# More expert-value blocks as full float32 products, and side-token dot products moved from the u stage into the v stage

## The reference, cut to what matters

```python
def peer(x, w_q, sub_keys, u, v):                 # once per layer, T = 256 tokens, D = 1024
    q = (xt @ w_q).reshape(T, 8, 2, 128)
    s = einsum('thpd,pnd->thpn', q, sub_keys)     # scores of 2 x 128 sub-keys per head
    sv, si = top_k(s, 16)
    cand = sv[:, :, 0, :, None] + sv[:, :, 1, None, :]
    cv, ci = top_k(cand.reshape(T, 8, 256), 16)
    experts = (i1 * 128 + i2)                     # 8 x 16 = 128 experts of 16384 per token
    gates = softmax(cv)
    a = gelu(einsum('td,tkd->tk', x, u[experts])) * gates
    return einsum('tk,tkd->td', a, v[experts])
```

## Time and profile before

| | us |
|---|---|
| median of 3 runs | 1658.11 (1657.31 to 1663.31) |
| the profiled execution, its own time | 1663.31 |
| its span, first to last instruction | 1661.5 |
| PE busy | 1628.2 (98%) |
| DVE busy | 1323.9 (80%) |
| ACT busy | 651.8 (39%) |
| POOL busy | 500.2 (30%) |

### The profile page before, as it was taken

How to read it: one execution, slowest core, us unless ns; L and a number is a source line. 1 busy time by engine, 2 the same in 40 slices (tenths; PEclk the granted TensorE clock), 3 DMA queues, 4 the chain that set the end, 5 groups by cost and what they waited for, 6 DMA issues and landing times.

```text
span 1661.5 us, 28025 instructions
## 1 busy us (share of the span) xinstructions
PE 1628.2 (98%) x10822; PEld 1574.3 (95%) x10822; DVE 1323.9 (80%) x2543; ACT 651.8 (39%) x1179; POOL 500.2 (30%) x342
## 2 busy tenths in 40 slices
PE   9999999999999999999899999999999999999978
PEld 8978999999999999999788899999999999999976
DVE  6985795899997887877666749869899877877864
ACT  5553211333334444544535431123333344444542
POOL 5741002434332434342003200124343223434400
PEclk9999999999999999999999999999999999999999
DMA  7544558999998999997733246699999989999971
GB/s 246 211 143 153 181 200 290 337 335 342 341 345 320 351 347 359 350 351 267 285 117 116 90 163 202 199 337 343 335 347 342 351 314 353 350 357 348 348 240 51
DMA packets 126724, 459.30 MB, mean 276 GB/s; under 512 B 14272, under 2 KB 14784, under 8 KB 126336
## 3 DMA queue, kind: packets, MB, share of 16 engines
q1 hardware_dynamic: 85248, 307.42, 51.7%
q0 software_dynamic: 37312, 135.41, 21.9%
q10 hardware_dynamic: 4032, 14.68, 2.5%
HBM read 455.23 MB, written 1.05 MB: 275 GB/s over the span
## 4 chain that ended last, share of the span: by engine, by line
PE 77%; DVE 16%; DMA 4%; ACT 1%; issue 1%; SPq 0%; DVEq 0%; ACTq 0%
PE work L707 18%; PE y L847 8%; PE work L847 7%; PE work L727 7%; PE work L852 5%; PE y L852 5%; PE work L730 4%; PE y L838 4%; PE y L860 4%; PE work L860 3%; DVE y L1988 3%; PE work L788 3%; PE y L1162 3%; DMA raw<-v 2%; PE y L816 2%; DVE big L1686 2%
## 5 line engine op out<-in xcount | busy, mean ns | idle before, releaser
L707 PE MATMUL work<-columns,raw 128*128 128x192 f32 x2752 | 457.5, 327 | 0.0
L707 PEld LDWEIGHTS work<-columns,raw 128*128 128x128 f32 x2752 | 446.0, 190 | 0.0
L614 DVE TENSOR_TENSOR low<-raw,high 128x1024 fp32r<-128x1024 f32 x266 | 331.0, 1247 | 75.6 <-ACT high L1228 75.4
L1228 ACT ACTIVATE high<-raw 128x1024 fp32r<-128x1024 f32 x282 | 295.0, 1048 | 55.2 <-PE work L707 19.8
L677 POOL DMA_INDIRECT big<-v,picks x128 | 208.5, 1629 | 348.8 <-DVE big L1904 275.6
L677 POOL DMA_INDIRECT big<-u_rows,picks x128 | 182.2, 1423 | 289.3 <-DVE big L1822 272.3
L1489 ACT ACTIVATE xT<-big 128x192 fp32r<-128x192 f32 x210 | 74.2, 361 | 256.5 <-PE work L852 201.6
L1904 DVE SCALAR_TENSOR_TENSOR big<-big,side_hid 128x1024 f32<-128x1024 f32 x126 | 161.3, 1280 | 0.6
L1822 DVE SCALAR_TENSOR_TENSOR big<-big 128x1024 f32<-128x1024 f32 x128 | 152.8, 1219 | 0.0
L727 PE MATMUL work<-xT,high 128*128 128x384 f32 x672 | 136.5, 344 | 0.0
L847 PE MATMUL y<-xT,high 128*128 128x384 f32 x584 | 134.7, 352 | 1.5 <-DVE xT L1875 1.3
(11 more groups left out here) (252 smaller groups left out, 2585.2 us busy)
## 6 DMA issues: line engine op xcount, KB each, us to landing
raw<-u SPq DMA_DIRECT2D x256, 512.0 KB, 5.6
raw<-v SPq DMA_DIRECT2D x256, 512.0 KB, 6.7
raw<-wq SPq DMA_DIRECT2D x32, 512.0 KB, 3.8
raw<-conv_in SPq DMA_DIRECT2D x14, 512.0 KB, 4.6
aux<-ln_par ACTq DMA_DIRECT2D x9, 512.0 KB, 9.2
raw<-conv_out SPq DMA_DIRECT2D x8, 512.0 KB, 4.1
raw<-mla_out SPq DMA_DIRECT2D x8, 512.0 KB, 4.6
big<-diag ACTq DMA_DIRECT2D x6, 512.0 KB, 6.1
```

The source lines that it names most:

```text
L614: ops.tensor_tensor(low_at(c), raw_at(c), high_at(c).bitcast(F32), ALU.subtract).then_inc(low_made[RAW_SLOT[c]], 1)
L707: mm = nc.tensor.matmul(out_, raw_at(c)[:, k * P:(k + 1) * P], x_full[:, k, :], start=(k == 0), stop=(k == KD - 1))
L1228: A(high_at(c), raw_at(c), ACT.Copy).then_inc(high_made, 1)
```

## The change

`EARLY` goes from 33 to 37 and `CHOSEN_AT` with it from 30 to 34, so 45 pairs are left. `FULL_PAIRS` becomes every odd pair (22 of 45, before 26 of 47). Whole u blocks are then 37 + 1 + 44 = 82 per layer, before 86. `PAIR_OF` follows from the number of pairs: batches now also stand at split pairs (10, 12, ... 20 and 32, 34, ... 42), where before all stood at whole ones. In v every fifth block at two offsets is whole: 46 per layer, before 23 (3, 6, 8, 11, 13, ... 113, 116).

Of the 64 dots per layer, 26 stay in u, in odd pairs from 7 to 41. The other 38 stand at v blocks 2 to 42, the side gelu at block 45 (before 2), and the 64 sums at blocks 47 to 113, 1.0625 blocks apart (before 4 to 113, 1.734 apart). The gathers' order on POOL is unchanged.

```diff
-EARLY = 33
+EARLY = 37
-CHOSEN_AT = 30
+CHOSEN_AT = 34
@@
-FULL_PAIRS = {2, 4, *PAIR_OF}
+FULL_PAIRS = range(1, PAIRS, 2)
 MERGED = PAIRS - len(FULL_PAIRS)
+EARLY_DOTS = 26
 DOT_PAIRS = {}
-for _d in range(SIDE_ROWS):
-    DOT_PAIRS.setdefault(2 + _d * (PAIRS - 4) // SIDE_ROWS, []).append(_d)
-SIDE_GELU_AT = 2
+for _d in range(EARLY_DOTS):
+    DOT_PAIRS.setdefault(7 + 2 * (_d * 18 // EARLY_DOTS), []).append(_d)
+V_DOTS = SIDE_ROWS - EARLY_DOTS
+SIDE_DOTS_AT = {2 + _d * 11 // 10: EARLY_DOTS + _d for _d in range(V_DOTS)}
+SIDE_GELU_AT = max(SIDE_DOTS_AT) + 3
@@
-FULL_V = [_n for _n in range(FIRST_COLUMNS, COLUMNS - LAST_COLUMNS) if _n % 5 == 3]
+FULL_V = [_n for _n in range(FIRST_COLUMNS, COLUMNS - LAST_COLUMNS) if _n % 5 in (1, 3)]
@@
                 for c in range(v0, end - TAIL):
+                    if c - v0 in SIDE_DOTS_AT:
+                        side_dot(layer, SIDE_DOTS_AT[c - v0])
```

## The result

| | before | after |
|---|---|---|
| median, us | 1658.72 (1657.31 to 1663.31) | 1707.85 (1705.53 to 1710.18) |
| ratio | | 1.0291 (95% interval 1.0266 to 1.0317) |
| span of the profiled execution | 1661.5 | 1708.9 |
| u stage, layer 0 / 1 | 351.9 / 351.9 | 349.6 / 349.6 |
| first 100 v blocks | 235.9 / 235.9 | 245.3 / 244.8 |

The change makes the kernel 2.9% slower. The last three lines are counted from PE's records in order of time: u is from its first product to the first of v; in v each block has 16 records, so the first 100 blocks end where record 1601 starts, and the 20 blocks end with the last column product. Per layer u gains 2.3 us, the first 100 v blocks lose 9.4 and 8.9, the next 20 lose 17.5 and 17.1. Their sum over both layers, 48, is close to the 47.4 us by which the span grew. So about two thirds of what v loses stands in the last 20 of 120 blocks.

A forecast was written before the change was run, and what follows sets the result against it. PE was taken to bound u and v except v's ends, with transfers the second limit. Terms 6.3 + 0 + 14 + 5 = 25 per layer, 50.6 for two, on 1658.1 gave 1709 us; range 1672 to 1765.

The forecast's parts named there:

- Bound and whole blocks: u and v: PE-bound except v's ends; whole blocks cost 0.33 us more each, -1.3 in u, +7.6 in v, +6.3 per layer.
- Later pairs and batches: u pairs: later start and batches in split pairs taken as 0, bounds 0 and 16 us; four fewer whole blocks -1.3.
- Dots moved into v: v blocks 2 to 113: gathers exceed a 390 GB/s queue limit, net +14 us per layer, bounds 0 and +51.
- Slots and end of v: End of v: whole blocks hold slots that DVE, ahead, waits for; +5 us per layer, bounds -8 and +14.
- A: v: queues keep up, so only PE's extra work and the end remain; 1681 us, chance 0.23.
- B: v: queues are full already and stay at 351 to 360 GB/s; 1775 us, chance 0.15.
- C: Ends of v, blocks 98 to 119: less DVE work removes all 15.0 us of waits, not slower; 1656 us, chance 0.07.
- D: u pairs: DVE in crowded split pairs stops PE; 1709 + 16 to 32 = 1733 us, chance 0.07.

The follow-up runs named there:

- e1: The kernel before with only the v table changed, 46 whole v blocks per layer instead of 23: 1694.78 us, ratio 1.0198.
- e6: The kernel before with only the u tables changed (37 early whole blocks, odd pairs whole), all 64 dots still in u: 1662.95 us, ratio 1.0012.
- e11: The kernel before, v whole only at every eighth block from 3 to 91, `CHOSEN_AT` 32 instead of 30: 1637.57 us, ratio 0.9859.
- e12: e9 with each v gather moving 32 rows instead of 128, so side results are not valid: 1666.23 us, ratio 1.0017 to before.
- e9: The changed kernel with no v block whole from 96 on: 1678.32 us, ratio 1.0106 to before.
- e3: The changed kernel with the five added whole v blocks from 96 on split again: 1683.16 us, ratio 1.0129 to before.
- e4: The changed kernel with ACT and DVE never looking more than 3 blocks ahead in v: 1682.01 us, ratio 1.0124 to before.
- e5: The kernel before with one more whole v block per layer, block 116: 1679.98 us, ratio 1.0110.
- e7: The kernel before with no whole v block from 98 on: 1641.22 us, ratio 0.9874.
- e2: The kernel before with only the dots moved, 26 in u and 38 in v, gelu and sums later: 1685.84 us, ratio 1.0144.

## Why the prediction was right, and where it was not

The time, 1709 against 1707.85, was met, and that it was met so closely is luck. Two of its terms were wrong in opposite directions, by about 11 us per layer each, and cancelled. The direction, the whole blocks' price and the place of the waits were foreseen; how the rest of the loss splits was not.

*Bound and whole blocks: right.* PE's paces came out as worked out, and e1 shows 5.8 us for 19 added whole blocks up to 100, 0.31 each where 0.33 was taken. 7.6 for all 23 stands.

*Later pairs and batches: nearly.* Taken as -1.3 and 0; measured -2.3. The cost of the crowded pairs is real (e6), but only with the dots left in u. "PE's waits show none there worth it" overlooked 0.8 us for the choice, though that does not account for the rest by itself (e11).

*Dots moved into v: mis-sized.* The step said +14 per layer, from a ceiling of 390 GB/s. The plateau is 409, and the term measures 3.6 and 3.1 us up to block 100 beside whole blocks (e1 against the changed kernel); the bytes of the v gathers alone are worth 4.8 and 4.3 (e12 against e9). At 409 the prediction's own formula gives 1.018/0.409 = 2.49 against 2.42, +0.07 x 67 = 5 and +0.05 x 41 = 2, less a head start of 5: 2. So the formula comes near the measured size with the right ceiling; the 5 us row with 419 had been nearer than the 20 us row scaled by the share. The Trainium skill's 358 GB/s for one core's HBM share ("DMA: Bandwidth & Descriptors", Bandwidth) is passed by the 403 held from 540 to 760 us here; its 425 for a large transfer with the neighbour idle is close. Two slips of the prediction change nothing: its own formula gives an estimate of +45 per layer at 358 GB/s, not +46, and 23 of the 40 slices of the earlier trace rows move 314 GB/s or more, not 24.

*Slots and end of v: mis-sized the other way.* The step said +5 per layer, bounds -8 and +14; measured +17, of which 1.3 are PE's own work on four whole blocks: 16, outside its bounds. The place and the mechanism were named (block 116, DVE ahead of the slot), but the wait behind 116 was 9.0 us, not at most 6.5: after the low part of block 120 DVE also makes those of 121 and 122 before it has `hid` of 119, without which the last group can't start. Beside that, the waits before blocks 104 and 110 were not in the sum: the transfers that they hang on, behind whole blocks 98 and 106, took 10.2 and 7.0 us. Full queues and held slots meet there: in e1, with the same whole blocks and emptier queues, PE has no gap before 104 and 1.2 to 2.1 us at 109 and 110. Of the 16 us in layer 0, 13.0 are PE's longer gaps (19.6 against 6.6), and the rest is nearly all products that run slower for a few us behind a gap. e3, e4, e5 and e7 show the slots' part one by one; e5 puts 9.7 us per layer on block 116 alone (19.3 for both).

*Rivals.* A (queues keep up) was nearer on its own term than the forecast, but its 1681 left out the end. B is refuted by 403 GB/s over 220 us, where it took 351 to 360. C's place was right, and whole blocks there do spare DVE work that it can't carry (e9), but they make more waits than they take. D did not show in the changed kernel; e6 shows it exists.

How e1's and e2's losses add up: 33.0 and 24.1 us over their own runs of before; together 57, less 4.6 for u, 52.5, against 49.1. How the 16 us at the end split between slots and DVE is not settled, since taking the slots' part away uncovers DVE's (e9).

## What to carry to other kernels

A buffer kept by one consumer until it is done is priced at the place where another engine looks ahead furthest: count the steps between its release and the in-order engine's next wait for it. Reducing an engine's busy share is worth nothing by itself; here ACT and DVE became less busy and the kernel slower. A table of ratios along a stage (whole or split, one in five) should be looked at separately for its end, where lead, slots and side work change. A total that comes out right does not prove its terms: measure each piece.

## What the runs showed of the hardware

One core moved 403 GB/s over 220 us at a DMA share of 1.02, and 409 to 411 in stretches of 20 us at 1.03 (about half streamed blocks of 4 KB per partition, half gathered rows of 4 KB); before, the fastest stretch of that length in the earlier trace rows had 375. The share is not in proportion to the bytes: 351 GB/s scaled from 0.94 to 1.03 gives 385, where 409 were moved, and e12 has 0.88 with 268 GB/s. Transfers behind a whole block took up to 10.2 us with full queues, against 3.6 to 3.7 when the gathers were at their end. After gaps of 3.8 to 9.0 us PE's products ran slower for a few us (wide ones 1.28 us for four instead of 0.69), at a mean granted clock of 0.79 over the stretch from 800 to 820 us.
